# Hybrid pooling / state-space block with a mixture of experts: the residual written into PSUM by ScalarE, a stationary router table, a mix in quarters, and experts chosen by sorted eights

## The chip, the cores and the metric

One core of a Trainium2 chip. The metric is the device time of one launch in microseconds, given as the median of several runs; lower is better. The engines are TensorE (PE), VectorE (DVE), ScalarE (ACT), GpSimd (POOL) and SyncE (SP), which here mostly issues transfers. Each runs its own program in order and waits on semaphores for the others.

## The reference

256 latent tokens and 256 context tokens, width 1024, one layer, all in float32. A modulated RMSNorm, an input projection, pooling and a state-space scan give `cat`, and an output projection gives the mix. What matters for this change begins there:

```python
x = x + g1 * (cat @ w_out)                    # gated residual
h = modulate(rmsnorm(x, g_ffn), sh2, sc2)
s = sigmoid(h @ w_router)                     # 32 experts in 4 groups of 8
sel = s + b_router
# best group by the sum of its two best sel; the two best experts in it; ties go to the lower index
# gates: s of the two, divided by their sum
y = sum over the two experts of gate * (silu(h @ w_gate[e]) * (h @ w_up[e])) @ w_down[e]
out = rmsnorm(x + g2 * y, g_final)
```

`g1`, `sh2`, `sc2`, `g2` are rows of a product of the conditioning vector with `w_mod` plus `b_mod`. Each expert has three float32 matrices of 1024 x 512, 2 MB each: 6 MB per expert and 192 MB for the 32.

## The kernel before

Everything is hand scheduled: each engine has one written order of instructions, and named semaphores (`S("...")`) tie them. PSUM `ps` has 8 banks of 128 x 512. Tokens stand in NT = 2 blocks of 128, features in KD = 8 blocks of 128.

*Mix.* `mix_pool(n, ks)` adds the pooling half of the output projection to bank n (n = 2 * token block + column half), the loop over n and k at L857 the state-space half. A float32 matmul stands in the profile as two passes. In the middle of n = 3 the rows of token block 0 are turned.

*Residual and norm on DVE.* `residual(t, at, n)` multiplies the mix by `g1b` and adds it to `x2`; `scaled` makes `hn = x2 * A2b`, and `rows(t, half)` makes `h2P`, the rows which the experts take, 4 of the 8 feature blocks in one call. ScalarE squares `x2` and POOL makes `rstd2`.

*Router.* `turn_rows` transposes `hn` on TensorE in groups of four blocks (L838), ScalarE or DVE copies them to `xaT`, `logits(t)` multiplies each block with 32 columns of the router table, the tokens being the stationary side (L849). `logit(t)` scales them, ScalarE takes the sigmoid, DVE chooses: MAX8 over the 8 experts of each group (L1562), `first_best` (a maximum, a comparison times `rank`, a maximum, a comparison) once for the group and twice for the experts (L1568 to L1573). `rank` puts ties to the lower index. `msk` marks the chosen, `chosen` is the semaphore.

*Around it on TensorE, in this order.* logits, `start_output(0)` and `(1)` (the identity times `x2`, which puts the residual into banks 0 and 1, L830), `gate_product` (the bias row by a matmul of one row, L807, and the sum over partitions of `acc`, L808; it gives `g2b`), the counts of tokens per expert (L880, L881), `start_output(2)`, `gather(0)` and `gather(1)` (the rows of the first four experts, by the one-hot `Pm`, L894), `start_output(3)`, and then `four(0, ...)`: `gate_up` (L927, L928) for four experts with `gather(2)` and `gather(3)` in the middle of the first, `turn_hidden` (L943), `down` (L978). Later `scatter` adds the outputs to banks 0 to 3, on top of the residual.

*Transfers.* SP issues all loads of expert weights in one order (`gu_load` L246, `early_load` L251, `down_load` L258), each 1024 KB, each behind a wait for its buffer:

```python
            sp.wait_ge(S("xa_ready"), 3)
            down_load(sp, lambda j: j, 0, (2,))
            sp.wait_ge(S("gate_mm"), 1)
            early_load(sp, 1, w_up)
            sp.wait_ge(S("outs_started"), 1)
            sp.wait_ge(S("ss2_ready"), NT)
            down_load(sp, lambda j: j, 1, (3,))
            sp.wait_ge(S("h2_rows"), 2 * NT)
            down_load(sp, lambda j: j, 1, (2,))
```

After these come the refills. The first waits for `gu_half` 1, which TensorE raises when it is through the first four feature blocks of expert 0, the next for 2, 3, 4, and so on. The experts are worked on in fours, eight rounds with this input.

## Time and profile before

| | |
|---|---|
| median of 3 runs | 642.79 us (641.74 to 643.32) |
| the profiled execution | 646.29 us, span 644.2 us |
| mean granted TensorE clock | 0.964 of full |
| TensorE matmul busy | 590.5 us (92%) |
| VectorE busy | 196.5 us (31%) |
| ScalarE busy | 134.9 us (21%) |
| GpSimd busy | 49.2 us (8%) |
| moved by the transfers | 246.93 MB, 383 GB/s over the span |

The span goes from the first to the last instruction of the core. Some 187 us of it are the first part and the router, the rest is the stage of the experts. Durations in the rows are those of the profiled execution.

### The profile page before, as it was taken

The numbers are of one execution on the slowest core, as the hardware profiler recorded it, in microseconds if no ns is written. First come the engines' busy times: TensorE is split into PE (matmuls) and PEld (weight loads), VectorE is DVE, ScalarE is ACT, GpSimd is POOL, SyncE is SP. The second block draws the span as 40 slices with busy tenths as digits, with TensorE's granted clock in tenths as the row PEclk, the third lists the DMA queues.
The fourth block names the chain that finished last, engine by engine and source line by source line (L and its number), as shares of the span: only waits on it lengthen the run. The fifth ranks groups of instructions, "written<-read, shape, count | busy, mean of one in ns | idle before, by whom it ended". The sixth has DMA issues, their size and how long they took to land.

```text
span 644.2 us, 9383 instructions
## 1 busy us (share of the span) xinstructions
PE 590.5 (92%) x3790; PEld 247.9 (38%) x3790; DVE 196.5 (31%) x428; ACT 134.9 (21%) x238; POOL 49.2 (8%) x101
## 2 busy tenths in 40 slices
PE   1999999899999798999999899969988996999996
PEld 0454565464553242334334233423332342334331
DVE  7998499987630010002002001000100020001003
ACT  7761243041122111012111110202020111012112
POOL 3795000010000000000000000000000000000001
PEclk9999999899689999999999899979998998999999
DMA  8997785999879999999999999999999999999992
GB/s 311 422 398 268 273 300 185 371 397 410 365 272 420 421 365 423 421 421 386 425 422 421 423 422 422 423 420 422 423 422 422 423 418 423 422 421 419 419 402 88
DMA packets 43497, 246.93 MB, mean 383 GB/s; under 512 B 4664, under 2 KB 7368, under 8 KB 17616
## 3 DMA queue, kind: packets, MB, share of 16 engines
q1 hardware_dynamic: 41960, 243.93, 93.0%
q10 hardware_dynamic: 1160, 1.59, 0.7%
q0 software_dynamic: 352, 1.07, 0.6%
q8 instruction: 17, 0.28, 0.2%
q14 instruction: 8, 0.07, 0.0%
HBM read 244.46 MB, written 2.11 MB: 383 GB/s over the span
## 4 chain that ended last, share of the span: by engine, by line
PE 61%; DMA 16%; ACT 1%; DVE 0%; issue 0%; SPq 0%; POOL 0%; POOLq 0%; DVEq 0%
PE ps L927 26%; PE ps L978 17%; DMA wts<-in_w_up 16%; PE ps L894 4%; PE ps L900 3%; PE ps L857 2%; PE ps L943 1%; PE ps L763 1%; ACT ra L1211 1%; PE ps L819 1%; PE ps L830 1%; PE ps L779 1%; PE ps L808 1%; PE ps L807 1%; PE ps L959 0%; PE ps L849 0%
## 5 line engine op out<-in xcount | busy, mean ns | idle before, releaser
L927 PE MATMUL ps<-wts,ra 128*64 128x512 f32 x504 | 234.3, 618 | 23.3 <-DMA wts<-in_w_up 23.3
L928 PE MATMUL ps<-wts,ra 128*64 128x512 f32 x504 | 234.3, 618 | 0.0
L927 PEld LDWEIGHTS ps<-wts,ra 128*64 128x64 f32 x504 | 68.4, 141 | 168.5 <-issue 135.3
L978 PE MATMUL ps<-wts,ra 128*32 128x512 f32 x512 | 111.6, 593 | 0.7 <-DVE ra L1271 0.7
L978 PE MATMUL ps<-rc,ra 128*32 128x512 f32 x512 | 111.6, 593 | 0.0
L1271 DVE TENSOR_TENSOR ra<-ra,ps 128x256 f32<-128x256 f32 x32 | 13.5, 421 | 259.5 <-ACT ra L1217 259.5
L1211 ACT COPY ra<-ps 128x512 f32<-128x512 f32 x32 | 33.5, 1046 | 217.4 <-PE ps L928 217.4
L928 PEld LDWEIGHTS ps<-wts,ra 128*64 128x64 f32 x504 | 68.4, 141 | 0.0
L978 PEld LDWEIGHTS ps<-wts,ra 128*32 128x32 f32 x512 | 29.1, 110 | 74.1 <-issue 73.1
L1271 DVE TENSOR_TENSOR cb<-ps,ra 128x512 f32<-128x512 f32 x32 | 22.1, 691 | 102.7 <-PE ps L978 102.7
L1206 ACT COPY ra<-ps 128x512 f32<-128x512 f32 x32 | 18.7, 585 | 144.3 <-PE ps L894 144.3
L894 PEld LDWEIGHTS ps<-cb,ra 128*128 128x128 f32 x256 | 30.5, 195 | 13.4 <-issue 7.7
L537 POOL TENSOR_SCALAR small<-small 128x1 f32<-128x1 f32 x2 | 0.4, 224 | 430.1 <-ACT ra L1249 430.1
L894 PE MATMUL ps<-cb,ra 128*128 128x128 f32 x256 | 33.3, 284 | 0.0
L668 PE MATMUL ps<-ra,wts 128*128 128x512 f32 x64 | 29.6, 600 | 0.6 <-ACT ra L1096 0.6
L978 PEld LDWEIGHTS ps<-rc,ra 128*32 128x32 f32 x512 | 29.1, 110 | 0.0
L900 PE MATMUL ps<-cb 128*128 128x512 f32 x56 | 26.4, 593 | 0.0
L943 PE MATMUL ps<-cst,ra 128*128 128x128 f32 x128 | 21.0, 287 | 4.4 <-ACT ra L1211 4.4
L943 PEld LDWEIGHTS ps<-cst,ra 128*128 128x128 f32 x128 | 13.4, 140 | 25.8 <-issue 19.5
L563 PE MATMUL ps<-wts,sil 128*32 128x512 f32 x96 | 13.4, 646 | 8.2 <-DMA wts<-in_w_mod 8.2
L1271 DVE TENSOR_TENSOR cb<-cst,ut 128x256 f32<-128x256 f32 x16 | 6.7, 421 | 45.2 <-PE ps L894 43.8
L668 PEld LDWEIGHTS ps<-ra,wts 128*128 128x128 f32 x64 | 11.4, 190 | 13.5 <-issue 11.8
(238 smaller groups left out, 537.3 us busy)
## 6 DMA issues: line engine op xcount, KB each, us to landing
wts<-in_w_up SPq DMA_DIRECT2D x63, 1024.0 KB, 16.7
wts<-in_w_gate SPq DMA_DIRECT2D x63, 1024.0 KB, 15.0
rc<-in_w_down SPq DMA_DIRECT2D x28, 1024.0 KB, 21.2
wts<-in_w_down SPq DMA_DIRECT2D x28, 1024.0 KB, 17.4
wts<-in_w_mod SPq DMA_DIRECT2D x16, 1024.0 KB, 13.1
r<-in_w_mod SPq DMA_DIRECT2D x6, 1024.0 KB, 5.9
wts<-in_w_out SPq DMA_DIRECT2D x2, 2048.0 KB, 14.3
wts<-in_w_down SPq DMA_DIRECT2D x6, 512.0 KB, 16.4
```

What stands on the lines that cost most here:

```text
L563: mm = pe.matmul(ps[32 * j:32 * j + 32, bank, :], silc[:, k, :], w[:, 512 * j:512 * j + 512], start=False, stop=(k == KD - 1))
L668: mm = pe.matmul(ps[:, 4 + q % 2, :], WBs[:, k, P * q:P * q + P], hT[:, k, :], start=(k == 0), stop=(k == KD - 1))
L857: mm = pe.matmul(ps[:, n, :], cat[:, 4 + k, P * (n // 2):P * (n // 2) + P], wo_ssm[:, k, 512 * (n % 2):512 * (n % 2) + 512], start=False, ...
L894: mm = pe.matmul(o, h2P[:, t, k, :], Pm[:, t], start=True, stop=True, skip_group_check=True)
L900: pe.matmul(ps[:, 2 * t + h, :], PT[:, t, :], oS[:, 2 * h + t, :], start=False, stop=False, skip_group_check=True)
L927: pe.matmul(ps[0:64, 4 + b, :], st, gate_k, start=(k == 0), stop=(k == KD - 1))
L928: mm = pe.matmul(ps[64:128, 4 + b, :], st, up_k, start=(k == 0), stop=(k == KD - 1))
L943: mm = pe.transpose(ps[:, 6 + j % 2, P * f:P * f + P], gu[:, j % 2, P * f:P * f + P], ident)
L978: mm = pe.matmul(ps[32 * j:32 * j + 32, BANKS[n], :], hid[:, j, f, SLOTS * t:SLOTS * t + SLOTS], Wd[j][:, f, 512 * h:512 * h + 512], start ...
L1206: act.copy(xm[:, 2 * r:2 * r + 2], ps[:, GATHER[r], :].rearrange("p (k e s) -> p k e s", k=2, e=4)).then_inc(S("xm_ready"), 1)
L1211: act.copy(gu[:, j % 2, :].rearrange("p (f q) -> p q f", f=FC), ps[:, 4 + j % 2, :].rearrange("p (q f) -> p q f", f=FC)).then_inc(S("gu_co ...
L1271: return dve.tensor_tensor(o, a, b, op)
```

## The change

- `residual` goes to PSUM through two copies on ScalarE (`act.copy(ps..., x2)`) behind the copy of `g2b`; the four `start_output` matmuls are gone. `outs_started` is now raised by ScalarE, and TensorE waits for it ahead of its second round.
- The bias of the gate row is added by POOL (`mod_bias(1)`) behind the load of `brb`; `gate_product` loses its two matmuls of one row.
- `logits`: the router table is stationary, 32 columns in one of four column groups, 128 tokens move; the four partial sums, with experts on partitions, are copied to `lgp` by DVE and multiplied by `stack4` (four identities on top of each other), which adds and turns them.
- The last quarter of the mix (columns 256 to 511 of n = 3) has bank 7 for itself. `mix_pool(2, (0,))` moves ahead of the wait for `hp_ready`. DVE takes residual and `scaled` in pieces of 512, 512, 512, 256, 256 columns and starts behind n = 0. Block 1's last four feature blocks are turned in two pairs, both copied by DVE.
- `rows` takes any feature blocks, in five calls in place of four; only two blocks of token block 1 stand ahead of the choice. `rank` is made earlier.
- The two experts come from MAX8 over all 32 `sel` values and a second MAX8 over rank values, in place of two `first_best`.
- The gates' reciprocal goes behind the first slots, and two more calls of `rows` stand ahead of the number of passes.

```diff
-            sp.wait_ge(S("mix_mm"), 4)
+            sp.wait_ge(S("mix_mm"), 5)
...
-            sp.wait_ge(S("xa_ready"), 3)
+            sp.wait_ge(S("xa_ready"), 5)
             down_load(sp, lambda j: j, 0, (2,))
             sp.wait_ge(S("gate_mm"), 1)
             early_load(sp, 1, w_up)
-            sp.wait_ge(S("outs_started"), 1)
+            sp.wait_ge(S("outs_started"), NT)
...
-            sp.wait_ge(S("h2_rows"), 2 * NT)
+            sp.wait_ge(S("h2_rows"), 5)
...
             gp.dma_start(brb, b_router.rearrange("(a d) -> a d", a=1).broadcast_to([P, NE])).then_inc(S("br_in"), 16)
+            mod_bias(1)
...
-                pe.wait_ge(S("mod2_used"), 2 * KD)
+                pe.wait_ge(S("mod2_sum"), 4)
                 for h in range(2):
                     j = 2 + h
-                    pe.matmul(ps[:, 6 + h, :], ones[32 * j:32 * j + 1, :], modrow[32 * j:32 * j + 1, 2, :], start=True, stop=False)
-                    mm = pe.matmul(ps[:, 6 + h, :], ones, acc[:, 512 * j:512 * j + 512], start=False, stop=True)
+                    mm = pe.matmul(ps[:, 6 + h, :], ones, acc[:, 512 * j:512 * j + 512], start=True, stop=True)
...
+            pe.wait_ge(S("a2b_ready"), 1)
+            mix_pool(3, range(4), 7, slice(256, 512)).then_inc(S("mix_pool"), 1)
...
+                    mm = pe.matmul(ps[32 * q:32 * q + 32, 7 - t, 0:P], wrt[:, k, :], xaT[:, t, k, :],
+                                   start=(k < 4), stop=(k >= 4), skip_group_check=True)
...
+            mix_ssm(3, 3, slice(0, 256)).then_inc(S("mix_mm"), 1)
+            for half in range(2):
+                pe.wait_ge(S("xa_ready"), half + 1)
+                turn_rows(0, range(4 * half, 4 * half + 4), 4 + half)
+            mix_ssm(3, 7, slice(256, 512)).then_inc(S("mix_mm"), 1)
             pe.wait_ge(S("shift_copy"), 1)
-            turn_rows(1, 0)
+            pe.wait_ge(S("xa_ready"), 3)
+            turn_rows(1, range(0, 4), 6)
+            pe.wait_ge(S("xat_act"), 2)
+            pe.wait_ge(S("xa_ready"), 4)
+            turn_rows(1, range(4, 6), 4)
+            pe.wait_ge(S("xa_ready"), 5)
+            turn_rows(1, range(6, 8), 5)
             pe.wait_ge(S("wr_in"), 16)
-            logits(0)
-            turn_rows(1, 1)
-            logits(1)
-            start_output(0)
-            start_output(1)
+            logits(0, range(KD)).then_inc(S("logit_mm"), 1)
+            pe.wait_ge(S("xat_act"), 3)
+            logits(1, range(4))
+            pe.wait_ge(S("turned"), 2)
+            logits(1, range(4, KD)).then_inc(S("logit_mm"), 1)
+            for t in range(NT):
+                pe.wait_ge(S("turned"), t + 3)
+                pe.matmul(ps[:, 4 + t, 0:NE], lgp[:, t, :], stack4, start=True, stop=True,
+                          skip_group_check=True).then_inc(S("logit_mm"), 1)
             gate_product().then_inc(S("gate_mm"), 1)
...
-            start_output(2)
...
-            start_output(3).then_inc(S("outs_started"), 1)
...
             act.copy(g2b, ps[:, 6:8, :].rearrange("p a n -> p (a n)")).then_inc(S("g2_ready"), 1)
+            for t in range(NT):
+                act.copy(ps[:, 2 * t:2 * t + 2, :].rearrange("p a n -> p (a n)"), x2[:, t, :]).then_inc(S("outs_started"), 1)
...
-            first_best(one1, sel, rank, NE)
-            link(dve.scalar_tensor_tensor(sel.rearrange("p t e -> p (t e)"), one1.rearrange("p t e -> p (t e)"), -HUGE * 4,
-                                          sel.rearrange("p t e -> p (t e)"), ALU.mult, ALU.add))
-            first_best(one2, sel, rank, NE)
-            tt(msk, one1, one2, ALU.add).then_inc(S("chosen"), 1)
+            for t in range(NT):
+                ins = dve.max(two[:, t], sel[:, t])
+            link(ins)
+            for t in range(NT):
+                dve.scalar_tensor_tensor(one1[:, t], sel[:, t], two[:, t, 1:2], rank, ALU.is_ge, ALU.mult)
+            link(tt(one2, sel, two[:, :, 1:2].broadcast_to([P, NT, NE]), ALU.is_gt))
+            link(dve.scalar_tensor_tensor(one1.rearrange("p t e -> p (t e)"), one2.rearrange("p t e -> p (t e)"), 2.0 * NE,
+                                          one1.rearrange("p t e -> p (t e)"), ALU.mult, ALU.add))
+            for t in range(NT):
+                ins = dve.max(two[:, t], one1[:, t])
+            link(ins)
+            tt(msk, one1, two[:, :, 1:2].broadcast_to([P, NT, NE]), ALU.is_ge).then_inc(S("chosen"), 1)
...
             tt(Pm, iota4, columns(posx, slice(0, 4)), ALU.is_equal).then_inc(S("slots"), 1)
+            rows(1, slice(2, 4))
+            link(dve.reciprocal(best, best))
+            link(tt(gw, gw, best.unsqueeze(2).broadcast_to([P, NT, NE]), ALU.mult))
             link(dve.tensor_reduce(best[:, 0:1], ps[:, 5, 2 * NE:4 * NE], AX.X, ALU.max))
+            rows(0, slice(4, 8))
+            rows(1, slice(4, 8))
```

## Rows read from the trace of the kernel before

**Rows 1.** The page's shares of the chain that ended last, by line.
```profile
PE ps L927 26%; PE ps L978 17%; DMA wts<-in_w_up 16%; PE ps L894 4%; PE ps L900 3%; PE ps L857 2%; PE ps L943 1%; PE ps L763 1%; ACT ra L1211 1%; PE ps L819 1%; PE ps L830 1%; PE ps L779 1%; PE ps L808 1%; PE ps L807 1%; PE ps L959 0%; PE ps L849 0%
```

**Rows 2.** Windows: length, engines' busy us (instructions), granted clock, DMA share, GB/s.
```profile
165.00:181.00 16.00, 16.00 (x29) 6.83 (x29) 9.00 (x47) 1.27 (x2) 0.00 (x0) 0.50 0.75 297
174.00:188.00 14.00, 14.00 (x51) 7.10 (x52) 5.26 (x24) 2.18 (x3) 0.00 (x0) 0.73 0.52 182
188.00:214.00 26.00, 23.87 (x118) 8.71 (x118) 1.60 (x4) 6.22 (x8) 0.60 (x1) 1.00 1.01 419
226.00:229.00 3.00, 3.00 (x32) 0.91 (x28) 0.00 (x0) 0.00 (x0) 0.00 (x0) 1.00 0.53 156
256.00:260.00 4.00, 4.00 (x12) 1.12 (x10) 0.00 (x0) 0.00 (x0) 0.00 (x0) 0.57 1.02 424
```

**Rows 3.** Timeline of SP's issues: start us, us, line, what.
```profile
163.00 0.33 SPq L258 DMA_DIRECT2D rc<-in_w_down  x1
178.00 0.33 SPq L251 DMA_DIRECT2D cb<-in_w_up  x1
183.71 1.09 SPq L258 DMA_DIRECT2D rc<-in_w_down  x2
187.30 0.33 SPq L246 DMA_DIRECT2D wts<-in_w_gate  x1
```

**Rows 4.** The chain from 150 to 230 us: start us, us, what.
```profile
162.28 0.70 DVE rc L1271
...
163.68 2.70 PE ps L849 x16
166.38 3.57 PE ps L830 x4
169.96 2.00 PE ps L807 x2
171.96 2.01 PE ps L808 x2
...
178.72 1.81 PE ps L830 x2
180.53 2.29 PE ps L894 x16
...
187.26 1.98 PE ps L894 x16
...
200.11 13.45 DMA wts<-in_w_up
```

**Rows 5.** What TensorE waited for, 186 to 236 us: total us, times, longest.
```profile
PE ps L927 <- DMA wts<-in_w_up: 2.1, 1, 2.1
```

**Rows 6.** Timeline of VectorE while it chooses the experts.
```profile
167.85 0.23 DVE L1271 TENSOR_TENSOR cb<-cb 128x64 f32<-128x64 f32 x1
...
170.44 0.22 DVE L1568 TENSOR_REDUCE cb<-cb 128x2 f32<-128x64 f32 x1
...
172.88 0.75 DVE L1271 TENSOR_TENSOR cb<-cb 128x64 f32<-128x64 f32 x3
```

**Rows 7.** Groups by form, 117 to 190 us: busy us, mean ns, idle before.
```profile
L779 PE MATMUL ps<-rc,ra 64*32 64x128 f32 x256 | 5.8, 310 | 3.0 <-DVE ra L1271 2.6 <-issue 0.5
...
L521 POOL TENSOR_TENSOR cb<-cb,mr 1x512 f32<-1x512 f32 x2 | 2.5, 1264 | 73.8 <-DVE cb L1478 73.7
...
L1519 DVE SCALAR_TENSOR_TENSOR ra<-rc,small,ra 128x512 f32<-128x512 f32 x2 | 2.2, 1104 | 0.0
...
L1271 DVE TENSOR_TENSOR cb<-cst,ut 128x256 f32<-128x256 f32 x3 | 1.3, 425 | 5.6 <-PE ps L894 4.3 <-issue 1.2 <-DVE ut L1271 0.2
...
L1200 ACT COPY ra<-ps 128x1024 f32<-128x1024 f32 x1 | 1.0, 1012 | 10.9 <-PE ps L808 10.9
...
L1570 DVE SCALAR_TENSOR_TENSOR cb<-cb 128x32 f32<-128x32 f32 x4 | 0.8, 250 | 0.1
...
L1562 DVE MAX8 cb<-cb 128x8 f32<-128x8 f32 x8 | 0.6, 153 | 0.0
...
L1271 DVE TENSOR_TENSOR ut<-cb,ps 128x64 f32<-128x64 f32 x1 | 0.2, 220 | 4.3 <-PE ps L881 4.3
```

More of the change, by code:

```diff
@@ L515, in _, with mod_bias @@
             gp.dma_start(ctmp, w_router.rearrange("(p k) e -> p k e", k=KD)).then_inc(S("wr2_in"), 16)
-            def mod_bias():
-                gp.wait_ge(S("mod2_used"), KD)
-                for j in range(2):
+            def mod_bias(gate):
+                for j in (2 * gate, 2 * gate + 1):
                     a = acc[32 * j:32 * j + 1, 512 * j:512 * j + 512]
@@ L758, in _, with mix_pool @@
             mm.then_inc(S("pool_mm"), 1)
-            def mix_pool(n, ks=range(4)):
+            def mix_pool(n, ks=range(4), bank=None, cols=slice(0, 512)):
+                o = ps[:, n if bank is None else bank, 0:cols.stop - cols.start]
                 for k in ks:
-                    mm = pe.matmul(ps[:, n, :], cat[:, k, P * (n // 2):P * (n // 2) + P],
-                                   wo_pool[:, k, 512 * (n % 2):512 * (n % 2) + 512], start=(k == 0), stop=False)
+                    c0 = 512 * (n % 2)
+                    mm = pe.matmul(o, cat[:, k, P * (n // 2):P * (n // 2) + P], wo_pool[:, k, c0 + cols.start:c0 + cols.stop],
+                                   start=(k == 0), stop=False)
                 return mm
@@ L770, in _ @@
             mix_pool(1)
+            mix_pool(2, (0,))
             pe.wait_ge(S("hp_ready"), 1)
@@ L783, in _ @@
                 if m < 3:
[L784 removed]
+                    mix_pool(2, (m + 1,))
             mm.then_inc(S("y_mm"), 1)
[L786 removed]
             mix_pool(3, (0,))
@@ L792, in _ @@
             mm.then_inc(S("y_t"), 1)
-            mix_pool(3, (1,))
+            mix_pool(3, (1, 2, 3), cols=slice(0, 256))
             def scale_product():
@@ L856, in _ @@
                         pe.wait_ge(S("cat_ssm"), k + 1)
-                    mm = pe.matmul(ps[:, n, :], cat[:, 4 + k, P * (n // 2):P * (n // 2) + P],
-                                   wo_ssm[:, k, 512 * (n % 2):512 * (n % 2) + 512], start=False, stop=(k == 3))
-                    if n == 0 and k == 3:
-                        pe.wait_ge(S("a2b_ready"), 1)
-                        pe.wait_ge(S("shift_prod"), 1)
-                        pe.matmul(ps[:, 6, 0:NE], ones, cpart, start=True, stop=True).then_inc(S("shift_mm"), 1)
@@ L863, in _ @@
-                    if n == 3 and k == 1:
-                        turn_rows(0, 0)
-                        turn_rows(0, 1)
-                mm.then_inc(S("mix_mm"), 1)
-            pe.wait_ge(S("shift_copy"), 1)
-            turn_rows(1, 0)
-            pe.wait_ge(S("wr_in"), 16)
-            logits(0)
-            turn_rows(1, 1)
-            logits(1)
-            start_output(0)
-            start_output(1)
+                    c0 = 512 * (n % 2)
+                    mm = pe.matmul(ps[:, bank, 0:cols.stop - cols.start], cat[:, 4 + k, P * (n // 2):P * (n // 2) + P],
+                                   wo_ssm[:, k, c0 + cols.start:c0 + cols.stop], start=False, stop=(k == 3))
@@ new lines, in mix_ssm @@
+                return mm
+            pe.wait_ge(S("wo_ssm_in"), 16)
+            mix_ssm(0, 0).then_inc(S("mix_mm"), 1)
+            pe.wait_ge(S("shift_prod"), 1)
+            pe.matmul(ps[:, 6, 0:NE], ones, cpart, start=True, stop=True).then_inc(S("shift_mm"), 1)
+            mix_ssm(1, 1).then_inc(S("mix_mm"), 1)
+            mix_ssm(2, 2).then_inc(S("mix_mm"), 1)
+            mix_ssm(3, 3, slice(0, 256)).then_inc(S("mix_mm"), 1)
+            for half in range(2):
+                pe.wait_ge(S("xa_ready"), half + 1)
+                turn_rows(0, range(4 * half, 4 * half + 4), 4 + half)
@@ L1009, in _ @@
             four(0, False, True)
+            pe.wait_ge(S("outs_started"), NT)
             pe.wait_ge(S("passes_ready"), 1)
```

95 lines of the change are left out of this document (48 added, 47 removed).

## The prediction

> **What bounds the kernel now.** I read the chain that ended last first: the matmuls of the expert stage (L927, L978) lead it with 43%, and behind them stands one transfer, the incoming w_up, with 16% [rows 1]. So the second view is the windows table, with its last column. In the expert stage the transfers run at 419 GB/s with a DMA share of 1.01 (188 to 214 us): TensorE has pauses there (23.87 busy of 26), the transfers have none. Two stretches are different: 174 to 188 us has 182 GB/s, and 226 to 229 us has 156 GB/s [rows 2]. The stretch of 14 us lost 14 x (1 - 182/419) = 7.9 us of transfer, the other one 3 x (1 - 156/419) = 1.9 us.
>
> Then the queue: SP issues nothing from 163.3 us (the last of four loads after the mix) to 178.00, two loads at 183.71, and the first refill of an expert buffer at 187.30 [rows 3]. These wait, in this order, for gate_mm; for outs_started and h2_rows; for gu_half 1. So between the mix and the first half expert the program is late, and the transfers run dry. That it counts later is seen in the chain: it stands in "DMA wts<-in_w_up" for 13.45 us from 200.11 [rows 4], and TensorE was really idle for 2.1 us of it [rows 5]. From there on landing, products, refill and next landing hang together, so what the stream gains by 213.6 us the end gains.
>
> Before 187.3 the chain is TensorE in its program order [rows 4]: last product of DVE 162.28, end 162.98; a turn and 16 router passes to 166.38; start_output(0), (1) 3.57; the bias matmul and the product of the gate, 2.00 + 2.01, twice, to 177.97; counts to 178.72; start_output(2) 1.81; gathers 2.29; start_output(3) 0.86 to 183.68; four steps of gate_up to 187.26. DVE had chosen the experts at about 173.6 [rows 6] and waited 4.3 us for the counts [rows 7]. And the clock was at its lower level, 0.50, for 165 to 181 us, with TensorE busy all the time [rows 2].
>
> **The change, part by part.**
>
> Mix and turns. Until the mix nothing is removed: one mix_pool step moves into an idle stretch, the last quarter gets its own bank. The last half of the mix is cut into two quarters, 8 passes of 256 columns each. DVE now works in quarters: row block 0 is done before n=2 ends at about 156.4, then 3 x 0.70 + 3 x 0.43 + one rows() of 1.11 + 3 x 0.43 (rates of 0.425 for 256 columns and 1.104 for rows() [rows 7]; 0.70 per 512 columns [rows 4]) is 5.8, started at 156.5: the last product is done at 162.35 instead of 162.98. Gain 0.6.
>
> Router. Before, behind the last product: a turn 0.66, 16 passes in 2.70 (they fell to the lower clock) [rows 4], and the evacuation by DVE. Logits ended near 166.75. Now: turn of two blocks 0.35, copy 0.43, the four-column-group passes, a copy of 128 columns, the product with the stack table, the last logit. No row has this very form; 256 matmuls on small parts of the array took 5.8 us here, 0.023 each [rows 7], so 24 passes of 128 columns lie between 0.6 and the old 0.17 each = 4.0. By shape I am near the first: 0.7, of which half is ahead of the last turn. Two copies 0.6 together and the stack product 2 x 0.17 = 0.35, logit 0.25. Sum from 162.35: 2.0 to 5.0, I take 2.1: 164.4. The gate product can start at 164.1.
>
> Selection. `rank` leaves the path (0.17) and only a quarter of rows() stands there (0.55 for 1.10). Before, `sel` began at 167.85, 1.1 behind the logits; now 0.65 behind: 165.05. From sel to the group mask is unchanged, 170.44 - 167.85 = 2.6: 167.65. Then before two first_best of 1.2 and more, up to about 173.4 [rows 6]. Now four MAX8, two STT at 0.25, three tensor ops at 0.22, one STT at 0.22, links. MAX8 on 8 elements is 0.153 [rows 7]; on 32 it lies between that and 0.43 (the 256 column row). I take 0.18: 2.0 together, range 1.9 to 3.0. Chosen at 169.6, 4.0 earlier.
>
> Gate product and counts. The four passes of `start_output` (3.57), the two bias matmuls (4.0), and later 1.81 and 0.86 leave TensorE: 10.2 us of its line. The gate product alone is 2 x 2.01 at the lower clock: 164.1 to 168.1, finished before DVE has chosen, so it costs nothing; without that cover (DVE at no cost) it would be the bound by up to 1.5. Counts 0.75 to 0.95: 170.5. The bias is now added by POOL, 1.26 each [rows 7], in 151.7 to 154.9, more than 9 us before it is used. DVE runs its residual there; what that could cost DVE is between 0 and 2.5, and 0.7 of it is hidden by its wait for n=2. I take 0. The Trainium skill, GPSIMD Engine Reference, section Specifications, says GpSimd shares its SBUF interfaces with VectorE when the latter has two SBUF inputs; no row here shows them at work together. Were all 2.5 lost, the forecast would move by less than that, as below.
>
> Slots, ScalarE. posx 0.22, slots 0.42 and the hops between are 0.9: 171.4 [rows 7]. ScalarE copies g2b (1.01 [rows 7]) to 169.15 and then x2 into PSUM, twice. No row writes PSUM from ScalarE; with 1.01 per 1024 columns it ends at 171.2, before the first gather is there to be copied (173.3). At twice that price it would end at 173.2, still in time. So the residual in PSUM costs nothing on the path, and outs_started comes at 171.2 instead of 183.7.
>
> Gathers and the first half expert. From 171.45 TensorE runs 16 gather passes and, with no start_output(3) between, gate_up. At the upper clock this is 2.0 + 3.6 (187.26 - 183.68). At the lower one it is 3.8 + 7.2. In 256 to 260 us, behind a TensorE pause, the clock was 0.57 with gate_up passes running, and 1.00 after it; so this kind of work gets it back within some 4 us, at a price of half of that. I take gathers slow, 3.8, and 0.9 for the rest plus 0.2 of waits: first half done at 179.9. Bounds: 177.0 to 182.4. Gain against 187.26: 7.4 (4.9 to 10.2).
>
> Here a rule is weighed against the rows. The rows: busy TensorE, clock 0.50 for 16 us [rows 2]. The Trainium skill, TensorE: Matmul & The Clock Gate, section What's actually happening, says that throttled is the default and activity releases it; taken alone that speaks against the change, since it takes filler passes out of the line. Rows 2 agree only in part (16 us of such passes did not release it). By the rule the first half would be done at the late bound or after it, which is rival (a) below.
>
> **The transfers.** Loads in flight run out at about 174 as before, where the poor stretch of [rows 2] begins. Now 1 MB follows at 168.1 (gate_mm), 1 MB at 171.3 (outs_started), 1 MB at 175.3 (h2_rows 5: Pm to 171.8, then three rows() of 0.55 + 1.1 + 1.1 and three small ones). At 2.5 us per MB (1024 KB at 419 GB/s) they cover until 181.5. The first refill comes at 179.9, the second 5.6 later at 185.5, before the first one's 5.0 (a half of gate and one of up, 2 MB) is through at 186.5; later ones come every 3.4. So the whole 7.9 us closes. Landing of expert 3's last half: 213.6 - 7.9 = 205.7. TensorE reaches that point 7.4 earlier than at 211.5, so at 204.1: still in front, by 1.6. Gain = the smaller of 7.9 and 7.4 + 2.1 = 9.5: 7.9. The 226 us gap keeps its size, since it hangs at the same landing.
>
> The profiled execution took 646.29 with a span of 644.2; the median of the runs shown is 642.79, 3.5 less. Span forecast 636.3, profiled execution 638.4, and median 642.8 - 7.9 = 634.9.
>
> **Rivals.**
> (a) TensorE becomes the bound: the clock stays low through the first half expert and on into the second, 3.5 us more at half speed costing 1.75 each time. With 182.4 the gain is 4.9 + 2.1 = 7.0 (635.8), with one or two such stretches more 5.3 or 3.5: 637.5 to 639.3, in the middle 637. For: rows 2. Against: the same passes recovered at 260.
> (b) More: the second gap closes as well, 1.9: 633.0. Against: down_half hangs at the landing.
> (c) No change, 642.8: the filled gap is paid back, as the stream is limited in total by something else than its issues. Against: 419 GB/s flat on either side of the gap [rows 2].
> (d) Slower: the clock stays low through the whole first four experts. TensorE has 10.2 + 2.1 = 12.3 us to give if fast; half of each low microsecond is lost, so 24.6 us of low clock from 171.5 decide; with 32 us the loss is 16 - 12.3 = 3.7: 646.5. For: 16 us of it are in the trace. Against: those were not gate_up passes.
>
> **How the numbers follow.** Forecast 0.60, (a) 0.20, (b) 0.07, (c) 0.08, (d) 0.05. A difference of 0.3% (1.9 us) is about what this measurement can tell from none. Faster: 0.60 + 0.20 + 0.07 = 0.87; same 0.08; slower 0.05. The range takes the forecast, (b) and most of (a): 633.0 to 638.5.
>
> **What would show it.** Transfers at 415 or more in every window between 165 and 225; SP issues near 168, 171, 175 and 180; last product near 162.4, logits 164.4, chosen 169.6, slots 171.4; first half expert at 180. Wrong if the clock is low in 180 to 200, if ScalarE's PSUM copies are far over 1 us, or if MAX8 grows with its length.

## The result and the profile after

| | before | after |
|---|---|---|
| median, 15 runs each | 642.04 us (640.22 to 646.25) | 639.99 us (636.83 to 641.84) |
| ratio | | 0.9950, 95% 0.9932 to 0.9968 |
| profiled execution, span | 646.29, 644.2 | 638.43, 635.9 |
| mean granted TensorE clock | 0.964 | 0.974 |

The changed kernel is faster by 0.50% (0.32 to 0.68%), about 3.2 us; the two medians alone differ by 2.05 us, or 0.32%, the lower end of that interval. The forecast was 7.9 us faster, 634.9, with a range up to 638.5: the direction was right, the size was not, and the time lies outside the range. Yet the one profiled execution of the changed kernel is what was forecast (span 636.3, measured 635.9). The rest of this document is about that contradiction.

The windows of the changed kernel, with the columns of [rows 2]:

```profile
165.00:181.00 16.00, 11.49 (x57) 7.26 (x54) 11.31 (x58) 4.30 (x6) 0.30 (x1) 0.89 1.01 422
174.00:188.00 14.00, 14.00 (x72) 7.25 (x73) 4.66 (x20) 3.39 (x5) 0.00 (x0) 0.92 1.01 409
188.00:206.00 18.00, 16.48 (x80) 5.59 (x78) 0.84 (x2) 3.99 (x5) 0.60 (x1) 1.00 1.01 411
214.00:230.00 16.00, 16.00 (x142) 6.05 (x136) 3.10 (x5) 1.17 (x2) 0.00 (x0) 1.00 0.93 371
```

The stretch that had 182 GB/s in [rows 2] has 409. SP's issues answer to [rows 3] (start us, us, line, what):

```profile
163.62 0.33 SPq L260 DMA_DIRECT2D rc<-in_w_down  x1
167.75 0.33 SPq L253 DMA_DIRECT2D cb<-in_w_up  x1
170.65 5.65 SPq L260 DMA_DIRECT2D rc<-in_w_down  x2
180.10 0.33 SPq L248 DMA_DIRECT2D wts<-in_w_gate  x1
...
209.49 0.33 SPq L248 DMA_DIRECT2D wts<-in_w_gate  x1
...
219.30 0.80 SPq L260 DMA_DIRECT2D wts<-in_w_down  x2
```

The chain answers to [rows 4]: last product of DVE, passes of four column groups, MAX8 over 32 values, gathers, first half expert, the transfer, the first down.

```profile
163.17 0.43 DVE rc L1281
163.65 0.44 PE ps L834 x2
164.09 1.01 PE ps L841 x32
...
169.31 0.30 DVE cb L1612 x2
...
172.83 3.65 PE ps L901 x16
...
180.06 1.98 PE ps L901 x16
...
192.91 12.84 DMA wts<-in_w_up
205.79 0.64 PE ps L934
...
212.16 13.94 PE ps L985 x128
```

And TensorE's wait in 186 to 225 us, as [rows 5]: total, times, longest.

```profile
PE ps L934 <- DMA wts<-in_w_up: 1.5, 1, 1.5
```

Groups by form in 117 to 190 us (busy us, mean ns, idle before): three forms that no row of before had (L1210, L841, L1612), and the two that they are compared with:

```profile
L1210 ACT COPY ps<-rc 128x1024 f32<-128x1024 f32 x2 | 2.0, 1020 | 0.0
L841 PE MATMUL ps<-ra,wr 128*32 128x128 f32 x32 | 1.1, 276 | 0.0
L1208 ACT COPY ra<-ps 128x1024 f32<-128x1024 f32 x1 | 1.0, 1012 | 1.2 <-PE ps L812 1.2
L1612 DVE MAX8 cb<-cb 128x8 f32<-128x32 f32 x2 | 0.3, 186 | 0.0
L1592 DVE MAX8 cb<-cb 128x8 f32<-128x8 f32 x8 | 0.6, 152 | 0.0
```

Step by step, forecast and measured:

| step, us | forecast | measured |
|---|---|---|
| last product of DVE | 162.35 | 163.60 |
| gate_mm | 168.1 | 167.75 |
| experts chosen | 169.6 | 171.0 |
| outs_started | 171.2 | 170.65 |
| gathers begin | 171.45 | 172.83 |
| first refill | 179.9 | 180.10 |
| landing of expert 3's last half | 205.7 | 205.75 |
| span | 636.3 | 635.9 |

### The profile page after: what moved, and what is told of

The parts are those of the page before. It is cut to its first block, busy times and chain, and to the rows that moved or that the text cites. A ratio compares the mean times of both kernels' runs of the same rounds, so it can differ in the third digit from the quotient of the medians.

```text
span 635.9 us, 9413 instructions
## 1 busy us (share of the span) xinstructions
PE 577.3 (91%) x3798; PEld 245.1 (39%) x3798; DVE 198.1 (31%) x435; ACT 136.9 (22%) x240; POOL 52.5 (8%) x103
## 4 chain that ended last, share of the span: by engine, by line
PE 57%; DMA 16%; DVE 3%; ACT 2%; issue 1%; SPq 0%; POOL 0%; POOLq 0%; DVEq 0%
PE ps L934 26%; PE ps L985 17%; DMA wts<-in_w_up 16%; PE ps L901 5%; PE ps L907 3%; PE ps L950 1%; ACT ra L1221 1%; PE ps L768 1%; PE ps L823 1%; DVE rc L1281 1%; PE ps L785 1%; DVE ra L1281 1%; DVE cb L1488 1%; PE ps L966 0%; PE ps L935 0%
## 5 line engine op out<-in xcount | busy, mean ns | idle before, releaser
L768 PE MATMUL ps<-wts 128*128 128x512 f32 (+1 forms) x40 | 16.8, 555 | 0.0
```

Of the source, the lines that this page charges most:

```text
L768: mm = pe.matmul(o, cat[:, k, P * (n // 2):P * (n // 2) + P], wo_pool[:, k, c0 + cols.start:c0 + cols.stop], start=(k == 0), stop=False)
```

## The experiments

Two theories stand against each other. **A:** the gap of the transfers behind the mix sets the gain, and the trace of before shows it larger than it usually is. **B:** the gap always has that size, and the changed kernel gives part of it back later, where before does not. To compare runs, one number is formed from windows of 20 us: the transfer time lost in 160 to 320 us, the sum of 20 x (1 - GB/s / 422). 422 GB/s is what the filled stretches show. The table has it for every profiled execution, with the rates of two stretches: 174 to 188 holds the first gap, 214 to 230 the second.

| run | edit | ratio (95%) | span | 174:188 | 214:230 | lost |
|---|---|---|---|---|---|---|
| before | | 1 | 644.2 | 182 | 366 | 11.5 |
| b1 | none | 0.9979 (0.9952 to 1.0006) | 639.7 | 310 | 363 | 7.3 |
| b2 | none | | 639.4 | 366 | 325 | 7.2 |
| b3 | none | | 645.6 | 177 | 360 | 12.5 |
| after | | 0.9950 (0.9932 to 0.9968) | 635.9 | 409 | 371 | 3.8 |
| a1 | none | 0.9939 (0.9912 to 0.9966) | 634.9 | 401 | 389 | 3.1 |
| a2 | none | | 639.9 | 410 | 297 | 6.7 |
| a3 | none | | 639.0 | 418 | 314 | 5.4 |
| a4 | none | | 638.7 | 414 | 296 | 6.7 |
| k1 | before, residual by ScalarE | 0.9967 (0.9941 to 0.9992) | 638.7 | 345 | 388 | 6.6 |
| k4 | k1, bias by POOL | 0.9963 (0.9936 to 0.9989) | 639.2 | 363 | 371 | 6.3 |
| k3 | after, residual by TensorE | 0.9934 (0.9905 to 0.9963) | 636.6 | 410 | 372 | 3.6 |
| k5 | k3, bias by TensorE | 0.9949 (0.9923 to 0.9975) | 636.5 | 418 | 354 | 4.1 |
| k6 | after, old choice | 0.9959 (0.9931 to 0.9988) | 639.1 | 407 | 362 | 4.6 |
| k9 | after, old router | 0.9963 (0.9936 to 0.9991) | 638.4 | 410 | 377 | 4.8 |
| k8 | after, three loads late | 1.0020 (0.9997 to 1.0043) | 641.8 | 247 | 367 | 9.0 |
| k7 | after, downs split | 0.9904 (0.9870 to 0.9938) | 635.0 | 410 | 411 | 2.3 |
| k7 again | the same | 0.9955 (0.9933 to 0.9977) | 638.5 | 413 | 347 | 6.0 |
| k10 | before, downs split | 0.9988 (0.9956 to 1.0021) | 642.6 | 177 | 416 | 9.8 |
| k11 | k7, a turn moved | 0.9928 (0.9908 to 0.9948) | 637.2 | 419 | 355 | 4.4 |

Span less lost lies between 631.8 and 634.5 in all twenty rows, while the span itself goes from 634.9 to 645.6. The time lost by the transfers explains most of what separates these executions, whatever the kernel.

### The kernel before, three times more

No edit.

> The kernel before, unchanged, profiled again. Theory A (the profiled execution of before was a slow one: its clock fell to 0.50 from 165 to 181 us and made TensorE's line to the first refill 8 us longer than in most executions): this trace has a shorter stretch of low clock between 160 and 182 us, the first refill at 180 to 184 us instead of 187.3, the poor stretch of transfers loses 3 to 5 us instead of 7.9, span 640 to 642. Theory B (the gap is always there, and something else made that execution slow, or makes the changed kernel's usual executions slower than its profiled one): refill at 187 again, low clock again, 7 to 8 us of transfer lost, and the difference in span lies elsewhere. Timed: ratio 1.000 within 0.3%.

> A third trace of the kernel before. Theory A: again unlike the first, the clock high past 165 and the first refill at 182 to 184, transfers of 174 to 188 us at 280 to 330 GB/s, span 639 to 641. Theory B: like the first, refill at 187 and 182 GB/s. If the fall of the clock has no fixed place it may lie anywhere between 164 and 172, and the refill between 183 and 187.5 with it.

> A fourth trace of before. Of 64 timed executions of before about one in five shows a mean clock of 0.964 to 0.967 with a span of 643.5 to 645.7, the others 0.971 to 0.981 with 638.4 to 642. Theory A: at 0.964 to 0.967 this trace has the long low stretch and the refill at 186 to 188, otherwise a short one and the refill at 180 to 184.

The windows of 165:181 and 174:188, first of b1:

```profile
165.00:181.00 16.00, 15.53 (x50) 7.61 (x51) 11.97 (x58) 2.44 (x4) 0.00 (x0) 0.79 0.82 331
174.00:188.00 14.00, 14.00 (x68) 7.52 (x69) 5.47 (x23) 2.35 (x4) 0.00 (x0) 0.87 0.79 310
```

of b2:

```profile
165.00:181.00 16.00, 14.41 (x56) 6.02 (x56) 11.98 (x58) 2.44 (x4) 0.00 (x0) 1.00 0.94 374
174.00:188.00 14.00, 13.95 (x76) 6.92 (x78) 4.84 (x21) 3.41 (x5) 0.00 (x0) 1.00 0.93 366
```

and of b3:

```profile
165.00:181.00 16.00, 16.00 (x29) 6.83 (x29) 9.43 (x47) 1.27 (x2) 0.00 (x0) 0.50 0.77 307
174.00:188.00 14.00, 14.00 (x51) 7.14 (x50) 4.88 (x22) 2.18 (x3) 0.00 (x0) 0.72 0.51 177
```

The column to read is the granted clock. One program, four executions: 0.50, 0.79, 1.00, 0.50 in the same 16 us. At 0.50 TensorE's line sets the pace and the first refill goes out at 187.30 (b3: 187.24). In b1 the clock fell only at about 171 us, and there SP issues

```profile
172.33 0.33 SPq L251 DMA_DIRECT2D cb<-in_w_up  x1
179.36 1.09 SPq L258 DMA_DIRECT2D rc<-in_w_down  x2
182.95 0.33 SPq L246 DMA_DIRECT2D wts<-in_w_gate  x1
```

4.4 us earlier than in [rows 3]; in b2 the first refill is at 180.56, nearly as early as in the changed kernel and earlier than had been expected (182 to 187.5). The gap then costs 14 x (1 - 310/422) = 3.7 us and 14 x (1 - 366/422) = 1.9 us, in place of 7.9.

How often is which? In all series together, 130 executions of before have their span and mean clock on record. 23 have a clock of 0.964 to 0.967 and spans of 643.5 to 645.8 (median 644.2). The other 107 have a median span of 639.8, 93 of them at or below 642.0. The trace on which the forecast was made (0.964, 644.2) belongs with the 23. The mean clock divides them only roughly: nine of the 107 have spans of 643.5 or more too, and k10 below has the first gap in full at a mean clock of 0.971. The changed kernel has 30 executions, median span 637.75, from 634.9 to 639.9: none of them reaches 643.5. 639.8 - 637.75 = 2.05 in the usual case and 6.45 in 23 of 130 give a mean of 2.8; with all 32 executions at 643.5 or more in the upper group it is 3.1. Measured was 3.2 (2.1 to 4.4). Theory A holds for most of the missing gain.

### The changed kernel, four times more

No edit.

> The changed kernel, unchanged, profiled again. Theory A: the same as its first trace (first refill at 180, landing of expert 3's last half at 205.7, span 636 to 638). Theory B: refill and landing as before, but 1 to 3 us lost after 210 us in the long stage, by the rate of the transfers (below 420 GB/s). Timed: 0.993 to 0.997.

> A third trace of the changed kernel. Theory A (span = 632.5 to 633 plus the transfer lost from 160 us on): if the span is 637 to 639, the windows from 160 to 320 us show 5 to 6 us of lost transfer in place of 3 to 4, most of it in a second gap (220 us) that follows a later landing, or in front of the first refill when the low clock covers gathers and gate_up. Theory C (something in the long stage): 3 to 4 us lost before 320, and 1 to 3 us lost or waited after it.

> A fourth trace of the changed kernel, as the third: span above 637 goes with 5 us or more of lost transfer between 160 and 320 us (theory A), or with losses behind 320 us (theory C).

> A fifth trace of the changed kernel, as the third. With three more traces at least one should have a span above 637 (median of 27 executions: 637.7).

The first gap is closed in all five traces (401 to 418 GB/s). a1 (lost 3.1, landing at 204.49) is like the first trace or better. a2, a3 and a4 are not; the windows of a2:

```profile
206.00:212.00 6.00, 5.13 (x16) 1.46 (x16) 0.00 (x0) 0.00 (x0) 0.00 (x0) 0.72 1.03 434
214.00:230.00 16.00, 15.29 (x141) 5.24 (x139) 3.52 (x6) 0.65 (x2) 0.00 (x0) 1.00 0.76 297
```

and its chain there:

```profile
192.62 14.21 DMA wts<-in_w_up
...
208.19 0.84 PE ps L934
...
214.94 7.06 PE ps L985 x62
```

TensorE waited there (total, times, longest)

```profile
PE ps L934 <- DMA wts<-in_w_up: 2.8, 2, 2.5
```

The sequence: the last half of expert 3 lands at 206.83, 1.1 later than in the first trace, TensorE pauses for 2.5 us before it, the clock is low behind the pause, a gate_up pass takes 0.84 us in place of 0.42 for some 3 us, and the first down starts at 214.94 in place of 212.16: 1.1 of these 2.8 us are the landing, 1.7 the clock. a3 and a4 land at 206.75 and 206.85 and look the same; why they land later was not found. The reloads behind the downs are as late, and the second gap takes 16 x (1 - 297/422) = 4.7 us in place of 1.9. So three of five traces lose 2.2 to 2.9 more than the first in the very gap of which the prediction said that it "keeps its size". That this is B, something that only the changed kernel gives back, is not shown: b2, an unchanged before, has the same low clock and loses 3.7 us there. Compared as a whole, the five traces of the changed kernel lost 5.1 us on average and the two usual ones of before 7.3 and 7.2; that difference of 2.1 is the difference of the usual spans.

The length of the pause does not decide whether the clock falls: before paused 2.1 us [rows 5], k5 2.5 and b3 2.7, and they kept it; b2 paused 2.0 us and lost it (clock 0.72 in 206 to 212), k11 below lost it after 1.8 us. Nor is the pause longer in the changed kernel, with 0.5 to 2.7 us in five traces beside 2.0 to 2.7 in four of before.

### The parts on TensorE

k1 is the kernel before with the residual written by ScalarE (the waits for `outs_started` are as in the changed kernel):

```diff
-            start_output(0)
-            start_output(1)
...
-            start_output(2)
...
-            start_output(3).then_inc(S("outs_started"), 1)
...
             act.copy(g2b, ps[:, 6:8, :].rearrange("p a n -> p (a n)")).then_inc(S("g2_ready"), 1)
+            for t in range(NT):
+                act.copy(ps[:, 2 * t:2 * t + 2, :].rearrange("p a n -> p (a n)"), x2[:, t, :]).then_inc(S("outs_started"), 1)
```

> Before with one part of the change: x2 goes into PSUM by two ScalarE copies behind g2b, the four start_output matmuls are gone, the rest as before. TensorE's line loses 3.6 us ahead of the gate product and 2.7 behind the counts if the clock is low, half of it if not. Theory A: refill at 181 to 183, one half of the whole change's gain, 0.997 to 0.999. Theory B (gap always 7.9 us): gains 4 to 5 us, 0.993.

k4 adds the bias of the gate row on POOL:

```diff
+            mod_bias(1)
...
-                    pe.matmul(ps[:, 6 + h, :], ones[32 * j:32 * j + 1, :], modrow[32 * j:32 * j + 1, 2, :], start=True, stop=False)
-                    mm = pe.matmul(ps[:, 6 + h, :], ones, acc[:, 512 * j:512 * j + 512], start=False, stop=True)
+                    mm = pe.matmul(ps[:, 6 + h, :], ones, acc[:, 512 * j:512 * j + 512], start=True, stop=True)
```

> Before with both reliefs of TensorE: residual by ScalarE and the gate's bias by POOL; router, mix and choice as before. The second trace of before had the clock high until 170.9 us, TensorE's line ready at 172.3 and DVE's choice at 172.6, so that line is no bound there. Theory A (usual executions are those, the first trace was not): only the two start_output passes behind the counts are won, 1.8 + 0.9 us, first refill at 180 to 182, 1 to 2 us faster than before, 0.997 to 0.998. Theory B (TensorE's line is usually the bound): refill below 180, 4 us or more, 0.994.

k3 takes the changed kernel and gives the residual back to TensorE (the first diff in reverse); k5 gives the bias back too, and keeps only mix, turns, router and choice.

> The changed kernel with the residual put back on TensorE: start_output(0) and (1) ahead of the gate product, (2) behind the counts, (3) behind gather(1), no ScalarE copies. With a low clock the gate product ends at 171.7 instead of 168.1 and is now behind DVE's choice; counts 172.5, slots 173.4, gathers from 174.3, start_output(3) 1 to 1.8: first refill at 183 to 185. Both theories: transfers idle for 1.5 to 3 us before it, and 1 to 3 us slower than the changed kernel: 0.997 to 1.000 against before.

> The changed kernel with both reliefs of TensorE undone: four start_output and the one-row bias matmuls back, the mix in quarters, the stationary router table and the choice by MAX8 stay. Theory A: the clock decides. If it is high until the gate product is through, the product ends at 169.5 to 171 and the choice at 170.7 is the bound, refill at 180 to 181; if it is low, gate_mm comes at 176 and the refill at 185. Timed 0.995 to 0.998 against before. Theory B: refill at 185, always, and no gain left: 0.999 to 1.001.

The windows of k1:

```profile
165.00:181.00 16.00, 14.80 (x40) 7.18 (x41) 11.96 (x58) 4.30 (x6) 0.00 (x0) 0.57 1.01 402
174.00:188.00 14.00, 13.57 (x64) 7.84 (x66) 5.19 (x22) 3.39 (x6) 0.00 (x0) 0.79 0.93 345
```

k1 is the clearest of the four. Its clock was nearly as low as in the first trace (0.57), yet its first refill goes out at 182.71, as in b1 with its faster clock, and the gap has 345 GB/s. Seven of its ten executions have mean clocks of 0.965 to 0.969 and spans of 638.1 to 639.3, where the 23 of before with such clocks have 643.5 to 645.8. So the passes that leave TensorE are worth about 5 us when the clock falls early, as far as one trace and the mean clocks of the others tell, and hardly anything otherwise (639.0, 639.3 and 640.2 in the other three, against 639.8). In k4 TensorE has less to do still (10.93 us busy of 16 in 165 to 181), yet its first refill is at 182.88 (180 to 182 had been expected) and its ratio is k1's: 0.9963 beside 0.9967.

k3 and k5 show the other side. k3 lost nothing that can be measured (0.9934 against 0.9950, with intervals of 0.003; 1 to 3 us slower had been expected, a miss). k5, with all of the passes back on TensorE, has the ratio 0.9949 and the median span 637.65, where the changed kernel has 637.75. In the usual execution what DVE does earlier gives the whole gain: at the higher clock TensorE has done its extra passes by the time at which the choice is ready. Which of the two engines is last before the first half expert changes from execution to execution, and the prediction priced the change in one where it was TensorE by some 4 us.

There is a second reason why the relief bought nothing. The window of 165:181 of k3 and of k5:

```profile
165.00:181.00 16.00, 14.13 (x81) 7.46 (x73) 11.60 (x58) 2.74 (x5) 0.56 (x1) 1.00 1.00 411
165.00:181.00 16.00, 15.88 (x73) 7.58 (x73) 10.88 (x56) 3.36 (x5) 0.00 (x0) 1.00 1.01 420
```

The granted clock is 1.00 here, for 0.89 in the first trace of the changed kernel and 0.79 to 0.89 in the others. With the passes gone TensorE waits 3.4 us for the choice and has a low clock in the first gathers behind it; their 16 passes take 3.54 to 3.76 us in all five traces of the changed kernel. With the passes back they take 2.02 in both. From DVE's last product to the first refill it is 16.5 to 17.6 us in the five traces, 15.7 in k3 and 16.3 in k5: the kernels with more work for TensorE are no later. So about 1.6 us of the relief went into the low clock. In the kernel before the same passes did not always hold it (0.50 from 165 us in two traces), and k3 and k5 are one trace each.

### Router and choice alone

k6 is the changed kernel with the two calls of `first_best` back in place of the MAX8 over 32 values; k9 has tokens stationary again and no `stack4` product:

```diff
-                    mm = pe.matmul(ps[32 * q:32 * q + 32, 7 - t, 0:P], wrt[:, k, :], xaT[:, t, k, :],
-                                   start=(k < 4), stop=(k >= 4), skip_group_check=True)
+                    mm = pe.matmul(ps[:, 7 - t, 0:NE], xaT[:, t, k, :], wrt[:, k, :], start=(k == 0), stop=(k == KD - 1))
```

> The changed kernel with the experts chosen by the two first_best again, nothing else. DVE's choice comes 1.5 us later (3.2 for 1.7), all behind it too: first refill at 181.6 in place of 180.1. Theory A (what counts is how long the transfers are dry, and in the changed kernel they are dry for nothing): the three loads issued in between cover until 181.5, TensorE's lead of 1.6 us at the landing shrinks to nearly none: same time as the changed kernel within 0.5 us. Theory B (TensorE's and DVE's line is the bound from there to the end): 1.5 us slower, plus 0.0023 on the ratio.

> The changed kernel with the old form of the logits: tokens stationary, 32 columns of the table moving, sums straight on token rows in banks 7 and 6, no copy of partial sums and no product with the stack (the gate product waits for DVE's two logits, since it writes the same banks). Behind the last turn 16 + 4 passes of 0.117 to 0.17 each for 0.5 + two copies + the stack: logits 0.3 to 1.0 later. Theory A: hidden, the same time as the changed kernel within 0.3 us unless the low clock begins earlier with it. Rival (the router table's new form is what brought the gain): 2 us slower, 0.998.

k6's first refill is at 179.72, not the 181.6 expected: DVE does take 1.2 us more from its last product to the choice, but in this execution that product was done 2.0 us sooner. k9's first refill is at 181.99, 1.9 later than in the changed kernel. Up to 188 us that is covered, since three loads lie ahead of it (410 GB/s in 174 to 188), but 180 to 200 us has 385 GB/s for the changed kernel's 406, which is 1.0 us more lost; "within 0.3 us" was a miss. Median spans are 638.4 (k6) and 638.8 (k9) against 637.75. Both intervals overlap that of the changed kernel (0.9959 and 0.9963 against 0.9950); each part may be worth 0.6 to 1 us or nothing, and the times don't decide it.

### Does the end follow the transfers or TensorE?

k8 leaves every engine's work as it is and issues the three loads between mix and refill behind the first refill:

```diff
-            sp.wait_ge(S("gate_mm"), 1)
-            early_load(sp, 1, w_up)
-            ...
             sp.wait_ge(S("gu_half"), 1)
             gu_load(sp, 0, 4, 0)
+            sp.wait_ge(S("gate_mm"), 1)
+            early_load(sp, 1, w_up)
+            sp.wait_ge(S("outs_started"), NT)
+            sp.wait_ge(S("ss2_ready"), NT)
+            down_load(sp, lambda j: j, 1, (3,))
+            sp.wait_ge(S("h2_rows"), 5)
+            down_load(sp, lambda j: j, 1, (2,))
```

> The changed kernel with the three loads between the mix and the first refill (up of expert 2 early, down of 3 and of 2, 3 MB) issued behind the first refill's gate load; TensorE, DVE and ScalarE as before. Theory A (end = a constant of about 634 us less nothing, plus the microseconds in which the transfers are dry after 160 us): queues run dry at 174 until 180, 5.5 to 6 us lost, and the whole comes back in the end: span 640.5 to 642, 5 to 6 us slower than the changed kernel, 1.002 to 1.005 against before. Rival (TensorE's line from the first gathers to the end is what counts, the transfers catch up): refill at 180 as before and the end as well, 0.995.

```profile
174.00:188.00 14.00, 14.00 (x73) 6.57 (x74) 3.64 (x19) 3.22 (x5) 0.00 (x0) 0.95 0.64 247
```

In this window of k8 TensorE and its clock are as after (14.00 busy, 0.95), its first refill is even earlier (179.09), and still the gap costs 14 x (1 - 247/422) = 5.8 us. The chain shows where it comes due:

```profile
191.89 19.26 DMA wts<-in_w_up
```

The half lands at 211.15 in place of 205.75, and the median span is 642.95, 5.2 over that of the changed kernel. This is the mechanism of the prediction, tested alone: what the stream loses by this landing, the end loses.

### The second gap

k7 splits the first reload of the down matrices: the first halves are issued when the first four experts' products with them are through, the second halves behind `down_half`. `cb_zero` and `vec_in` are semaphores whose first use is over by then.

```diff
+                        if first and f == 0 and n == 3:
+                            mm.then_inc(S("cb_zero"), 1)
                         if f == 1 and n == 3:
                             mm.then_inc(S("down_half"), 1)
...
-            downs(1, 0)
+            sp.wait_ge(S("cb_zero"), 2)
+            down_load_one(sp, lambda j: 4 + j, 0, range(4), "vec_in")
+            sp.wait_ge(S("down_half"), 1)
+            down_load_one(sp, lambda j: 4 + j, 1, range(4), "down_in0")
```

> The changed kernel with the second gap attacked: the first reload of the down matrices is split, rows f = 0 of all four are issued when the first four's f = 0 products are through, 3.5 us ahead of down_half. Theory A: the dry stretch between 216 and 221 us (1.2 to 2 us lost there) shrinks below 0.5, and 1.2 to 1.8 us come off the end: 0.992 to 0.993 against before. Rival (the landing bounds, the gap is only where slack shows): no change, 0.995.

> The split reload again, in more executions. Theory: with the f = 0 rows issued at once behind the first quarter of the products, the second gap is at most 0.5 us without the low clock behind the landing and 1.5 to 2.5 us with it. Median span 635 to 636.5, 0.990 to 0.993 against before. If its executions are as wide as those of the changed kernel (634.9 to 639.9), the low clock behind the landing is not hidden by the split.

> The kernel before with the first reload of the down matrices split, and nothing else. Theory A: the two gaps lie behind one another and add up, so the second one's 2 us are won here too: 0.996 to 0.998 against before. Rival (the second gap is only where the first one's delay shows, closing it pays only once the first is closed): 0.999 to 1.001.

k7's window is

```profile
214.00:230.00 16.00, 16.00 (x138) 6.01 (x132) 3.10 (x5) 1.17 (x2) 0.00 (x0) 1.00 1.02 411
```

so the gap is closed (0.4 us lost), the span is 635.0, and the ratio is the best of all, 0.9904. Timed again, beside other executions of before, it was 0.9955 with a median span of 637.6 (635 to 636.5 had been expected, a miss), and the profiled execution had a low clock behind the landing:

```profile
206.00:212.00 6.00, 5.94 (x20) 1.86 (x20) 0.00 (x0) 0.57 (x1) 0.00 (x0) 0.72 1.00 422
214.00:230.00 16.00, 15.90 (x146) 5.97 (x146) 3.13 (x6) 0.59 (x1) 0.00 (x0) 1.00 0.97 347
```

Here the split issues came 2.1 us later (217.80 in place of 215.68), behind the low clock, and the gap was open again by 16 x (1 - 347/422) = 2.8 us. k10, the same split on the kernel before, closed the second gap too (416 GB/s) and had the first in full (177 GB/s): 9.8 lost, span 642.6, which is 1.6 under the group of 644 with the same low clock. Over all its executions it can't be told from before (0.9988), so that the two gaps add up is seen in this trace alone.

k11 tries to fill TensorE's pause: the turn of the first experts' hidden rows moves ahead of the second half of expert 3.

```diff
+                    if turn_ahead and k == 4:
+                        turn_hidden(i, 2)
```

> The split reload, and the turn of expert 2's hidden rows (4 transposes, 0.66 us) done in TensorE's pause ahead of the second half of expert 3 instead of behind it. Theory: the pause shrinks from 1.5 to 2.5 us to 0.9 to 1.9, the clock falls behind it in fewer executions: median span 0.2 to 0.8 below the split alone, spread narrower. Rival (the clock falls for another reason than the pause, or the split hides it already): same as the split alone within 0.3 us.

The pause was 1.8 us, with 2.0 in the trace of k7's second run, and the clock fell all the same (0.72 in 206 to 212). Its ratio of 0.9928 stands beside 0.9955 for k7, timed together with it; the intervals overlap (0.9908 to 0.9948, 0.9933 to 0.9977); its median span, 635.55, is the lowest but for that of k7's first series (635.35). So the turn filled 0.2 us of the pause at most and did not hold the clock in the one trace; whether it falls more seldom is open. Whether k11, k7 or the changed kernel is the fastest stays open: they were not all timed together, and they differ by less than the two series of k7 do.

## Why the prediction was right and wrong

**What bounds the kernel: right.** The end follows the time that the transfers lose up to the landing of expert 3's last half. k8 shows it with no engine's work changed, and the table over all kernels agrees. Rival (c), a stream limited in total, is out: a gain was measured, and the filled gap has 401 to 418 GB/s. Rival (d) is out: none of 30 executions is slower than the usual one of before by more than 0.1 us.

**"So the whole 7.9 us closes": right for its trace, wrong for the median.** This is the step that failed. The gap does close, in all five traces. But 7.9 is its size when the clock falls at 165 us. The prediction saw that its profiled execution was 3.5 us over the median, wrote it down, and took the whole 7.9 off the median nevertheless. Those 3.5 us were the sign that the usual execution has a smaller gap: 3.7 us in b1 and 1.9 us in b2. The mis-sized term: 7.9, measured 3.7 and 1.9 in the two usual executions of before that were traced, and 8 in those like the first trace. Taken off the usual span of 639.8 these would have given 636.1 and 637.9, with 637.75 measured. The forecast could have been seen to be too low: a median of 634.9 is a span of about 632.9, and 631.8 to 634.5 is what the table leaves when no transfer time at all is lost. That the one profiled execution had the forecast span (635.9 for 636.3) is in part luck: it was among the faster ones, with the second gap at its small size. The median of 639.99 lies beside the 637.5 to 639.3 of rival (a), but not by its mechanism.

The row behind it is the clock, 0.50 for 16 us [rows 2], which the prediction read as a property of the program. It is one of the outcomes: the onset was 165 us in two traces of before, 171 in one, and in one it did not fall in 165 to 188 at all. The Trainium skill, TensorE: Matmul & The Clock Gate, section What's actually happening, says that the count of slow matmuls at the start of a kernel differs from run to run of the same kernel, and puts that penalty below 1% of a typical kernel. Here the difference comes in the middle of the kernel. Its size agrees, with 644.2 - 639.8 = 4.4 us, or 0.7%; it is more than the whole change is worth.

**"The 226 us gap keeps its size": wrong in three traces of five.** It hangs at the landing, as argued, and in a2 to a4 that came at 206.8 for 205.7; it hangs also at the low clock behind TensorE's pause: 4.1 to 4.8 us in place of 1.9. The prediction had "TensorE still in front, by 1.6" (measured 1.5 in the first trace, 2.5 in a2) and did not ask what a pause does: sometimes it is followed by half the clock for 3 us in the very passes that the next reload waits for. That happens in before as well (b2), so it does not by itself make the gain smaller. Rival (a) had a low clock in gate_up as its cause too, but in the first half expert, where it was back in time (refill at 180.10, not 182.4).

**TensorE's relief of 10.2 us: right as to the line, wrong as to when it counts.** It saves about 5 us in the executions with an early low clock (k1), and nothing that can be measured otherwise (k3, k5). The prediction weighed whether taking passes out of the line would let the clock fall. The gathers were slow, as it assumed (3.65 us for 3.8), and gate_up had the full clock from its start; with the passes left in they took 2.02 (k3, k5).

**DVE's side: right within 1.4 us.** Chosen at 171.0 for 169.6, from three terms. The last product was 1.25 late; from there to the logits it took 2.7 for 2.1 (the terms that the prediction lists add up to 2.3); the choice took 0.5 less than forecast, with MAX8 over 32 values at 0.186 us for the assumed 0.18. The column-group passes were near the lower bound (1.01 us for all 32 in the chain). What was late was made up by gate_up at the full clock, so that the refill came 0.2 late.

**The 1.25 us of the last product are no term of the sum.** The whole stretch lay later in that execution: with the same kernel the last product was done at 162.93, 162.27, 163.16 and 162.02 in a1 to a4, so in two of them on the forecast of 162.35. **The POOL bias** did slow DVE, for which the prediction took 0 out of 0 to 2.5. POOL and DVE of the changed kernel:

```profile
153.61 3.16 POOL L522 TENSOR_TENSOR cb<-cb,mr 1x512 f32<-1x512 f32 x2
154.00 1.64 DVE L1281 TENSOR_TENSOR ra<-rc 128x512 f32<-128x512 f32 x1
156.28 1.04 DVE L1281 TENSOR_TENSOR rc<-rc,ra 128x512 f32<-128x512 f32 x1
```

and the same two products in k5, where POOL is idle then, with DVE's wait behind them:

```profile
152.50 0.69 DVE L1289 TENSOR_TENSOR ra<-rc 128x512 f32<-128x512 f32 x1
153.83 0.69 DVE L1289 TENSOR_TENSOR rc<-rc,ra 128x512 f32<-128x512 f32 x1
...
156.24 0.69 DVE L1289 TENSOR_TENSOR rc<-ps,ra 128x512 f32<-128x512 f32 x1 [0.99 <-PE ps L858]
```

0.95 + 0.35 = 1.3 us on DVE, and POOL's two additions take 3.16 in place of 2.5 [rows 7]. The products between them that read PSUM stay at 0.68. This agrees with the rule of the GPSIMD Engine Reference, section Specifications, in the Trainium skill, which the prediction quoted and priced at nothing. But without it DVE waits 0.99 us for n = 2 of the mix, so most of it is hidden: from the start of the stretch (152.55, 151.05) to the end of the last product it is 11.05 us in the changed kernel and 10.87 in k5. The 0 was right within 0.2 us, by the cover that the prediction named.

**ScalarE into PSUM: right.** 1.02 us per 1024 columns, with 1.01 for the other direction; outs_started at 170.65 for 171.2.

## What to carry to other kernels

Before a stretch of one trace is priced, see whether that execution is a usual one: if it is 3.5 us over the median and the gain that is hoped for is 8, the difference is probably part of the gap, and only what the usual execution has may be taken off the median. Price a change in the resource that runs dry, and when two engines could each make a transfer late, take the later of the two in each case rather than the one which the trace happens to show. When work is taken off an engine that then waits for another one, ask what its clock does in the wait: here the passes behind it took 3.65 us in place of 2.02.

## What the runs showed of the hardware

- The same instructions in the same order had TensorE's clock at its lower level (0.50 of full, 1.2 GHz) from 165, from 171 or not at all in 165 to 188 us. What decides it was not found.
- TensorE busy without a pause stayed at that level for 16 us in two traces of before (before, b3), and in a2 gate_up passes behind a pause of 2.5 us were at 0.84 us each for some 3 us and then at 0.42 again.
- At TensorE's pause before the last half of expert 3 the clock fell in six traces (pauses of 1.8 to 2.7 us: b2, a2, a3, a4, k7 again, k11) and stayed full in seven with pauses of the same lengths (before, b1, b3, k3, k5, k6, k10). What decides it was not found.
- The 16 passes of the first gathers took 3.54 to 3.76 us in the changed kernel, where TensorE had waited 3.4 us shortly before, and 2.02 us in k3, k5 and b2, where it had waited 1.7, 0 and 1.1 us.
- A DVE product of 128 x 512 with two inputs in SBUF takes 0.69 us alone and 1.64 or 1.04 beside a POOL addition over one partition; with one input in PSUM it takes 0.68 in both cases.
- 32 passes of 128 columns in four column groups took 1.1 us.
